# Two modulation blocks moved between the layers, attention outputs multiplied one step later, and a window mask added on TensorE

## What is computed

```
# first block, twice (l = 0, 1): x and ctx are 256 tokens of 1024 values each
shift, scale, gate = split(sc @ w_ada + b_ada, 3)          # "modulation": 3072 values
h = rmsnorm(x, norm_w) * (1 + scale) + shift               # same for ctx
... = split_cols(h @ w_in)                                 # branches a, b, c
x = x + gate * merge(y_a, y_b, y_c, ...)                   # gate is used only at a layer's end
# branch a: log_sigmoid of the forget gates, cumulative sums and maxima over time, then exps
# second block, layer 0: 8 heads of dense attention, 8 heads of window attention
s = jnp.where(|k_abs - q_abs| <= 128, s * scale, -1e30)
p = softmax(concatenate([s, sink_col]))[..., :-1]          # one sink value for each head
# second block, layer 1: 8 latent heads, 8 heads with a position bias (masked too)
x = x + attention(...) @ w_out; x = x + cross_attention(...); x = x + swiglu(...)
```

## Time and profile before

| | us |
|---|---|
| median of 3 runs | 2383.32 (2382.74 to 2385.16) |
| the profiled execution | 2380.97, of which the span is 2379.0 |
| TensorE busy | 2317.4 |
| VectorE busy | 1348.8 |
| ScalarE busy | 1062.1 |
| granted clock of TensorE, mean | 0.997 |

### The profile page before, as it was taken

One profiled execution on the slowest core, in us unless ns is written; L12 is line 12 of the kernel. 1 busy time (PEld: TensorE's weight loads), 2 busy tenths in 40 slices (PEclk: granted clock), 3 DMA queues, 4 the chain that ended last, 5 costly groups with the idle time before them and its releaser, 6 DMA issues.

```text
span 2379.0 us, 37311 instructions
## 1 busy us (share of the span) xinstructions
PE 2317.4 (97%) x15652; PEld 2059.9 (87%) x15652; DVE 1348.8 (57%) x2571; ACT 1062.1 (45%) x2058; POOL 235.9 (10%) x248
## 2 busy tenths in 40 slices
PE   8999999999999999999999999999989999999998
PEld 7888878999877988889999999999878888978887
DVE  6544433567754222465465766346766876666875
ACT  5433322354542222344443545445455554565553
POOL 0000000212201011000002230110100110100110
PEclk9999999999999999999999999999999999999999
DMA  7422134222134222223233223447223554323544
GB/s 295 164 73 72 71 127 175 72 72 72 54 124 153 86 72 96 81 80 134 89 142 125 89 90 124 153 156 242 92 100 109 186 181 180 121 79 123 179 174 145
DMA packets 52631, 294.52 MB, mean 124 GB/s; under 512 B 9008, under 2 KB 15408, under 8 KB 21168
## 3 DMA queue, kind: packets, MB, share of 16 engines
q1 hardware_dynamic: 52464, 292.15, 34.4%
HBM read 288.98 MB, written 3.41 MB: 123 GB/s over the span
## 4 chain that ended last, share of the span: by engine, by line
PE 82%; DVE 11%; ACT 5%; issue 1%; DMA 1%; POOL 0%; DVEq 0%; SPq 0%; ACTq 0%; POOLq 0%
PE PS L546 80%; DVE wl L2129 2%; PE PS L550 2%; ACT TM L1472 2%; DVE wl L2131 1%; DVE TM L2110 1%; ACT TMG L1472 1%; ACT wh L1482 1%; DVE TM L2118 1%; DVE HY L2118 1%; DMA raw<-in_wpk 1%; DVE colS L2118 1%; DVE colS L2639 1%; DVE TMG L2118 0%; DVE colS L2114 0%
## 5 line engine op out<-in xcount | busy, mean ns | idle before, releaser
L546 PE MATMUL PS<-HY,wh 128*128 128x512 f32 (+3 forms) x4944 | 1280.3, 342 | 13.6 <-DVE HY L2118 5.7
L546 PEld LDWEIGHTS PS<-HY,wh 128*128 128x128 f32 (+2 forms) x4944 | 848.0, 189 | 129.9 <-DVE HY L2118 10.9
L546 PE MATMUL PS<-HY,wl 128*128 128x256 f32 (+1 forms) x3000 | 926.4, 309 | 0.0
L2129 DVE TENSOR_TENSOR wl<-raw,wh 128x1280 fp32r<-128x1280 f32 (+2 forms) x249 | 365.3, 1467 | 472.1 <-ACT wh L1482 472.0
L546 PEld LDWEIGHTS PS<-HY,wl 128*128 128x128 f32 x3000 | 567.7, 189 | 30.0
L546 PE MATMUL PS<-wh,HY 128*128 128x256 f32 x2916 | 551.4, 286 | 3.6 <-ACT TM L1472 2.5
L1472 ACT ACTIVATE TM<-PS 128x512 f32<-128x512 f32 (+4 forms) x383 | 189.6, 510 | 629.8 <-PE PS L546 520.2
L546 PEld LDWEIGHTS PS<-wh,HY 128*128 128x128 f32 x2916 | 461.8, 191 | 7.7 <-ACT TM L1472 5.2
L546 PE MATMUL PS<-wl,HY 128*128 128x256 f32 x1458 | 412.5, 283 | 0.0
L1482 ACT ACTIVATE wh<-raw 128x1280 fp32r<-128x1280 f32 (+2 forms) x249 | 299.8, 1204 | 244.5 <-PE PS L546 172.7
L546 PEld LDWEIGHTS PS<-wl,HY 128*128 128x128 f32 x1458 | 279.4, 192 | 0.3
(11 more groups left out here) (190 smaller groups left out, 1714.4 us busy)
## 6 DMA issues: line engine op xcount, KB each, us to landing
raw<-in_wpk SPq DMA_DIRECT2D x233, 1024.0 KB, 4.8
raw<-in_wpk SPq DMA_DIRECT2D x32, 704.0 KB, 4.0
TM<-in_wpk SPq DMA_DIRECT2D x6, 1024.0 KB, 17.3
X<-in_xin SPq DMA_DIRECT2D x1, 2048.0 KB, 15.3
Y<-in_wpk SPq DMA_DIRECT2D x2, 1024.0 KB, 21.0
Y<-bias_d SPq DMA_DIRECT2D x4, 512.0 KB, 9.7
raw<-in_wpk SPq DMA_DIRECT2D x3, 512.0 KB, 3.7
T<-in_tabs SPq DMA_DIRECT2D x1, 1216.0 KB, 5.7
```

Source lines behind the costliest of these rows:

```text
L546: return P.x.matmul(o, l, r, start=start, stop=stop)
L2129: D.x.tensor_tensor(wl[:, s, 0:c], raw[:, r, 0:c], wh[:, s, 0:c], ALU.subtract).then_inc(*lo_split.mark((u, 0)))
```

## The change

It moves two of the 24 modulation units, changes the order of `branch_a(1)`, and changes `heads` for 16 heads.

1. Units 22 and 23 leave `merge_b` of layer 0. They are loaded and multiplied between the layers: unit 22 behind the last matmul of `project_out(0)`, unit 23 behind `rstd_spread`. `ada_content` makes them hold the blocks 20 and 21 of the modulation (a part of the gate of layer 1). Their rows are copied by ScalarE. In the DMA queue they stand behind "gate" and behind the first "a_qk" of layer 1.
2. Fillers between the layers: 6, 6, 11 and 16 become 3, 6, 2 and none, with 5 new ones behind `o_gate(0)`.
3. In `branch_a(1)` ScalarE copies q and k before Abs, Exp and Ln, and VectorE splits the next unit before it waits for Ln; the transposed columns and their Exp move behind `o_gate(0)`. In both layers a one-element Ln is put ahead of the gates.
4. With 16 heads `high` and `normed_out` come one step later (`written`), and all but the last catch up in step 8.
5. In "ab" the window mask is no longer added by VectorE: for heads 8 to 15 TensorE adds it into PSUM, identity times mask, four matmuls of 128 columns in a step, behind the scores of both heads. ScalarE makes the fp32r copies of identity and mask in step 1. The scores of a bank may be overwritten after the exponential, no longer after the masking.
6. The sink's exponentials of two heads become one of four values; its maximum becomes a minimum of the negated values.

```diff
@@ plan_units
+        if l:
+            ada(22)
         qk(0)
+        if l:
+            ada(23)
         v(0)
@@
-            if l == 0:
+            if l == 0 and j < 2:
                 ada(ada_at(l, "b", 4 + j))
@@ TensorE, first_units and branch_a
                     if l:
-                        keep(11, 7)
+                        keep(2, 2)
...
                 if l:
-                    keep(16, 7)
+                    ada_turn(23)
                 for b in range(2):
                     v_half(0, b)
...
+                if l == 0:
+                    columns()
...
                 o_gate(0)
+                if l:
+                    keep(5, 4)
+                    columns()
@@ TensorE, modulation in merge_b
-                    if (q := ada_at(l, "b", j)) is not None:
+                    if (q := ada_at(l, "b", j)) is not None and q < 22:
@@ TensorE, project_out
-                        ada_turn(23)
+                        ada_turn(21)
                 if l == 0:
-                    keep(6, 7)
+                    ada_unit(22)
+                    keep(3, 6)
                     rstd_sums(1)
-                    keep(6, 7)
+                    keep(6, 6)
                     rstd_spread(1)
+                    ada_turn(22)
+                    ada_unit(23)
@@ heads
+        def written(s, n_heads):
+            last = n_heads // 2
+            return [p for p in ((s - 3,) if s < last else (s - 3, s - 2) if s == last else (s - 2,)) if p >= 0]
@@ TensorE, scores
+                    banded = stage[0] == "ab" and s >= 4
                     for qt in range(2):
                         for h in (2 * s, 2 * s + 1):
-                            t = mm(v2(s_bank(stage, h))[:, qt], qf(h, qt), kf(h))
+                            t = mm(v2(s_bank(stage, h))[:, qt], qf(h, qt), kf(h), qt == 0 or not banded, not banded)
...
+                    if banded:
+                        for h in (2 * s, 2 * s + 1):
+                            for qt in range(2):
+                                o = 128 * (1 - qt)
+                                t = mm(v2(s_bank(stage, h))[:, qt, o:o + 128], ident_r, window_r[:, qt], False, qt == 1)
+                            t.then_inc(*pe_step.mark((stage, "s", h)))
@@ freed
-                masked = stage[0] in ("ab", "cd") and h >= 8
+                masked = stage[0] == "cd" and h >= 8
@@ ScalarE, branch_a
+                act(small[:, 57:58], one[:, 0:1], ACT.Ln)
...
                     used("gate", l)
+                    qk(0)
                 act(a_gt, bank(2), ACT.Identity, ("a_gt", l), bias=vcol(f"bif{l}"))
@@ ScalarE, layer 1, H
                             act(H[0][:, k, tg:tg + 256], xs[:, k, tg:tg + 256], ACT.Identity, ("H", 1, k), bias=ada[:, 1, k, c:c + 1])
+                        if k == 1:
+                            row(23)
@@ ScalarE, heads
-                    if sink(h) is not None:
-                        for qt in range(2):
-                            act(colS[:, c + qt:c + qt + 1], vcol("sink", sink(h)), ACT.Exp, (stage, "sink", h), bias=nb[:, qt:qt + 1])
+                    if sink(h) is not None and h % 2:
+                        A.wait_ge(dve_step, (stage, "sink_arg", h))
+                        act(sink_pair(h - 1), sink_pair(h - 1), ACT.Exp, (stage, "sink", h))
...
-                    if s >= 2:
-                        for i in outputs_of(stage, s - 2):
+                    for p in written(s, n_heads):
+                        for i in outputs_of(stage, p):
                             high(i)
@@ ScalarE, between in self_attention
+                    if s == 1:
+                        A.wait_ge(consts_in, "second")
+                        act(ident_r, ident, ACT.Copy)
+                        act(window_r.rearrange("p q k -> p (q k)"), window, ACT.Copy, "window")
@@ VectorE, branch_a
                 used("gate", l)
+                if l:
+                    used("a_qk", 4)
+                    ada_turn(23)
                 D.wait_ge(act_step, ("a_ln", l))
@@ VectorE, heads
-                    if s >= 3:
-                        for i in outputs_of(stage, s - 3):
+                    for p in written(s - 1, n_heads):
+                        for i in outputs_of(stage, p):
                             low_out(i)
...
-                    if s >= 2:
-                        for i in outputs_of(stage, s - 2):
+                    for p in written(s, n_heads):
+                        for i in outputs_of(stage, p):
                             normed_out(i)
@@ VectorE, self_attention
-                heads(("ab", 0), 16, lambda h: 0.125, lambda h: winm if h >= 8 else None,
+                heads(("ab", 0), 16, lambda h: 0.125, lambda h: None,
```

More of the change, by code:

```diff
@@ L535, in head_rc, with sink_pair @@
             return colS[:, 8 * (h % 4) + 6 + qt:8 * (h % 4) + 7 + qt]
+        ident_r, window_r = HY[:, 0, 2048:2176], HY[:, 0, 2176:2432].rearrange("p (q k) -> p q k", q=2)
+        window = winm.rearrange("p q k -> p (q k)")[:, 128:384]
+        nsink = small[:, 40:48]
+        def sink_pair(h):
+            c = 8 * (h % 4)
+            return colS[:, c:c + 16].rearrange("p (a b) -> p a b", a=2)[:, :, 0:2]
         def stage_of(l):
@@ L1114, in scores @@
                 def scores(s):
+                    if stage[0] == "ab" and s == 4:
+                        P.wait_ge(act_step, "window")
                     for h in (2 * s, 2 * s + 1):
@@ L1506, in used, with row @@
                 convert(unit_after(place[tag, j]))
-            def head_row(q):
+            def row(q):
                 A.wait_ge(pe_step, ("ada_row", q))
@@ L1533, in branch_a @@
                 t0, N = lay(l)
[L1534 to L1545, removed]
-                A.wait_own(act_step)
-                act(a_g[:, 0], a_g[:, 0], ACT.Ln, ("a_ln", l), bias=1.0)
+                act(small[:, 57:58], one[:, 0:1], ACT.Ln)
                 def qk(h):
@@ L1562, in v_half, with columns @@
                         used("a_v", 4 * l + h)
-                qk(0)
+                A.wait_ge(projected, ("gate", l))
+                if l:
+                    A.wait_ge(pool_step, ("m_sum", l - 1, "c", 7))
+                    used("gate", l)
+                    qk(0)
+                act(a_gt, bank(2), ACT.Identity, ("a_gt", l), bias=vcol(f"bif{l}"))
+                if l == 0:
+                    used("gate", l)
+                A.wait_own(act_step)
+                act(a_g[:, 0], a_gt, ACT.Abs)
+                A.wait_own(act_step)
+                act(a_g[:, 0], a_g[:, 0], ACT.Exp, scale=-1.0)
+                A.wait_own(act_step)
+                act(a_g[:, 0], a_g[:, 0], ACT.Ln, ("a_ln", l), bias=1.0)
+                if l == 0:
+                    qk(0)
                 v_half(0, 0)
                 v_half(0, 1)
-                A.wait_ge(dve_step, ("a_cc", l))
-                for d in range(2):
-                    act(a_cm[:, 4 * d:4 * d + 4, :], bank(7 - d)[:, 16:32].rearrange("p (j h) -> p j h", h=4), ACT.Exp,
-                        ("a_cm", l), scale=-1.0)
+                def columns():
+                    A.wait_ge(dve_step, ("a_cc", l))
+                    for d in range(2):
+                        act(a_cm[:, 4 * d:4 * d + 4, :], bank(7 - d)[:, 16:32].rearrange("p (j h) -> p j h", h=4), ACT.Exp,
+                            ("a_cm", l), scale=-1.0)
+                if l == 0:
+                    columns()
+                else:
+                    A.wait_ge(pe_step, ("a_cols", l))
                 def o_gate(h):
@@ L1831, in project_out @@
                             used("w_out", 4 * l + k // 2)
+                    row(22)
                 else:
@@ L2077, in scalar_program @@
                             used("mem_k", 1)
-                        head_row(q)
+                        row(q)
                         if q == 1:
@@ L2283, in branch_a @@
                     tt(a_c[d], a_i[d], a_bs[d], ALU.subtract, ("a_rc", l))
-                used("a_qk", 4 * l)
+                if l == 0:
+                    used("a_qk", 0)
                 used("a_v", 4 * l)
```

52 lines of the change are left out of this document (31 added, 21 removed).

## The result

| | before | changed |
|---|---|---|
| median, us | 2384.10 of 4 runs (2382.74 to 2385.16) | 2365.03 of 4 runs (2364.05 to 2365.75) |
| profiled execution | 2380.97, span 2379.0 | 2365.31, span 2363.5 |

The ratio is 0.9919 (95% interval 0.9907 to 0.9931): 19.1 us less where 14.4 were forecast, and 2365.03 us where the forecast was 2368.9. Sign and mechanism held. One term, the heads of "ab", was too small by 3 us, two others by about 1 us each, and the profiled execution of before was a fast one for a reason that the prediction did not know.

A forecast was written before the change was run, and what follows sets the result against it. TensorE, busy 2317.4 of 2379.0 us, was taken to bound the kernel, plus 61.7 us standing still. Terms -3.2 - 2.2 - 5.4 - 3.6 = -14.4 us from 2383.32 gave 2368.9 us, range 2365 to 2376.5.

The forecast's parts named there:

- the heads of "ab": Masked steps of the "ab" heads: four of about 5.86 us become three at 4.5 and one at 4.0; -5.4 us.
- Merge b: Layer 0's merge b: two modulation units and two turns fewer on TensorE, 1.6 us each; -3.2 us.
- Units between the layers: Between the layers: two units and a turn replace 12 fillers, hidden by the chain to H; 0 us.
- Rival 2: Between the layers: unit 23's load lands late and delays layer 1; 2372.9 us in all, chance 0.06.
- Order of branch a: Layer 1, behind the gate products: q copied first, values start earlier, scores at 1069.4 instead of 1071.63; -2.2 us.
- the ring: 16-head steps: VectorE waits for ScalarE's denominator copy, ScalarE for the maxima behind; postponing the multiplication opens it, leaving the fullest engine.
- "cd": Heads of "cd": postponing alone brings four masked steps from 4.96 to 4.05 us; -3.6 us.
- offset of 2.35 us: Whole kernel: the median stands 2.35 us above the profiled run, added to the forecast for the changed kernel.
- The first, another ring: 16-head stages: a new ring through both engines keeps steps at 5.2 and 4.6 us; 2374.4 us, chance 0.14.
- The third: Between the layers: fewer fillers leave TensorE at 1.2 GHz, up to 31.5 us slower, 2400.4 us; chance 0.04.
- The fourth: Whole kernel: only the two saved units count, -3.2 us, the rest does nothing; 2380.1 us, chance 0.04.
- The Ln: Gate chains of both layers: the one-element Ln put ahead adds table loads but costs no time; 0 us.

The follow-up runs named there:

- heads-alone kernel: Only the 16-head edits (outputs one step later, window mask on TensorE, joined sink exponentials) against the kernel before: 2368.54 us, ratio 0.9947.
- outputs later: Kernel before with only the 16-head outputs one step later, VectorE still adding the mask: 2371.71 us, ratio 0.9958 against before.
- mask on TensorE: Kernel before with only the window mask of "ab" on TensorE, outputs multiplied in the same step: 2377.89 us, ratio 0.9983 against before.
- the last experiment: Changed kernel without one-element Ln and fillers ahead of layer 1's columns, VectorE split later, fp32r copies ahead of "ab": 2361.92 us, ratio 0.9906 against before.

## Why the prediction was right, and where it was short

The step that failed is the term of the heads of "ab", -5.4 us, which measured -8.4 (point 4): the right mechanism, with the steps behind the opened ring taken too long. The rest in the order of the sum:

1. **Merge b, -3.2**: measured 3.3. Right.
2. **Units between the layers, 0**: right, the first products moved by exactly what was won before. Unit 23 did not come late: at 1024.73 TensorE has no wait. Rival 2 falls.
3. **Order of branch a, -2.2**: 2.4 to the scores without the clock (3.5 less 1.1), 2.6 in the kernel with these edits alone. The rest of the 3.5 us, 1.1, is the stretch at half clock at 1034 of the earlier trace rows. I had taken it as a fixture of the place. The heads-alone kernel, with before's code up to there, doesn't have it, and ends the first products 1.1 us earlier than before does:

```profile
1034.00:1037.00 3.00, 2.76 (x14) 1.00 0.00 0
```

   Such a stretch lies between the layers in six of the twelve profiles, with either order of the code and with 39, 16, 11 or no fillers. Of two profiles of before both have it, of two of the changed kernel none; with three other kernels that have before's code there (heads alone, outputs later, mask on TensorE) none has. So it is taken as a matter of the execution, and the 1.1 us are not counted for the change; that the change makes it rarer isn't excluded by so few.
4. **"ab", -5.4**: the term that failed; measured -8.4. The mechanism was right (the ring opens and the fullest engine is left, TensorE), the steps were mis-sized, twice. First the count: I had three steps at 4.5 us and one without scores at 4.0, but TensorE multiplies the scores of a pair four outputs ahead, so behind the outputs of the fifth and the sixth pair there are none left, and two of the four steps have neither scores nor mask: 2.89 and 3.46 us (the second full on ScalarE), together 2.15 us below the 8.5 that I had for them. In before these steps were as long as the others (5.85): the ring set them, and it doesn't contain the scores. That hid the difference. Second, TensorE's own need: I added the masks, 0.65 us, to its busy time of 3.83 us in the earlier trace rows. The masks were nearly right (0.59). But a busy time holds the modelled end of each group that is followed by a wait; from start to start the groups of a step need 0.97 + 1.02 + 1.06 + 0.49 = 3.54 us, and with the masks 4.13. Against the 4.5 of the forecast that is 0.37 us in each of two steps. (I had ScalarE at 3.8 us; it was busy 4.13 and 3.89 in them.) The two together are 2.9 of the 3.0 us. The copies, +0.5, were right (0.49, won back in the last experiment).
5. **"cd", -3.6**: measured 4.4. The mechanism was right, the period was not one: the four steps took 3.62, 4.69, 3.83 and 3.82 us instead of 4.05 each, 15.96 us against my 16.2, and the step ahead of them, which I left out, goes from 4.30 to 3.80: 0.5 us. I had read the unmasked step as full on ScalarE (4.21 of 4.30); that it got shorter by the postponing shows that it was partly in the ring as well.
6. **The offset of 2.35 us** between median and profiled execution was carried over from before to the changed kernel, which is right only if both profiles were equally lucky. They were not: the pitch alone gives 3.8 us between them. Span against span the change is worth 15.5 us, median against median 19.1, and without the pitch the account above has 19.2; that this comes so near the 19.1 is partly chance, since neither the pitch nor the slow stretches of the other executions are known. So of the 4.8 us that the forecast missed by the account, 3.0 are "ab", 0.8 "cd", 1.1 the clock, 0.4 small terms, less 0.5 for the wait at 1645.
7. **Rivals.** The first, another ring, is refuted by steps of 4.13 and 2.89. The third was tested at full size, in one profile, and cost 1.5 us. The fourth falls with the heads alone (13.6 us less). The range ended at 2365, and 19.1 us less than the 2383.3 that it was built on are 2364.3, just below: its lower bound for "ab", -6.1, took 4.2 us for all four steps, and two of them took 2.89 and 3.46.
8. **The Ln.** Table loads of the changed kernel in branch a of layer 1, on ScalarE:

```profile
1036.48 1.28 ACT L1514 ACT_TABLE_LOAD   x1
...
1047.40 1.28 ACT L1514 ACT_TABLE_LOAD   x1
...
1049.35 1.28 ACT L1514 ACT_TABLE_LOAD   x1
...
1059.02 1.28 ACT L1514 ACT_TABLE_LOAD   x1 [0.44 <-PE PS L568]
```

   The Ln at 1036 brings a load, and Exp behind it still brings its own at 1047: loads rose from 15 to 18, and none cost time: from the start of the program to the scores of layer 0's branch a the starts shift by less than 0.1 us. The rule of the Trainium skill ("ScalarE: Activation LUTs", table sets) that Ln and then Exp need a single load, since one set holds both, disagrees with these four rows: Ln runs behind the loads at 1036 and 1049, Exp behind those at 1047 and 1059. Which set a load takes isn't in the trace. The other page of the Trainium skill that was weighed ("TensorE: Matmul & The Clock Gate", the gap between matmuls) gave 55.8 ns for 128 columns; the masks measured 0.11 to 0.15 us on fp32r operands. Its sum of 4.05 us for a step came near the measured 4.13 only because my 3.83 in it was too large by 0.29, nearly as much as 0.22 for the masks was too small (by 0.37).

## What to carry to other kernels

When a ring through two engines is opened, size the steps that follow by what each of them issues: list the groups of each step from start to start, and don't add new work to a busy time, which also counts the modelled end of a group ahead of each wait. Steps of equal length inside a ring need not hold equal work. And compare two profiles of the same program before a difference of a few microseconds is given to an edit: here one program's spans lay between 2377.7 and 2386.0 us.

## What the runs showed of the hardware

- One program, granted clock 1.00 and TensorE never idle: a pair of fp32r products of 512 and 256 columns starts every 346.7 ns or every 353.3 ns. In the twelve profiles one of the two holds from soon behind the start of a feed-forward layer to the wait in its middle, and one from soon behind that wait to its end; which one differs between executions of one program. Over the 345 us of the two feed-forward layers this is worth up to 6.6 us. What chooses it stays open; no kernel here was made to steer it.
- Stretches of 3.4 to 10.2 us at 1.2 GHz appear at places where TensorE waits, in some executions and not in others: between the layers in six of twelve profiles. In the heads they appear in all four profiles that keep the ring, and in none of the eight whose outputs come later.
- Four matmuls of 128 columns on fp32r operands took 0.59 us from start to start, four more 0.44 us.
